# Order of the attention pairs in the local phase: the context tile's four short pairs first

## The reference

```python
o_mla = dense_attention(q_mla, k_mla, v_mla, MLA_SCALE)               # 8 heads
o_swa = window_attention(q_swa, k_swa, v_swa, kswa_c, vswa_c, sink, HEAD_SCALE)   # 4 heads, +-128 tokens
o_na = neighbourhood_attention(q_na, k_na, v_na, kna_c, vna_c, rpb, HEAD_SCALE)   # 4 heads, 2-D window
x = residual_tail(x, concatenate([o_mla, o_swa, o_na]), ...)
```

## Time and profile before

| | |
|---|---|
| time, median of 3 runs (lowest, highest) | 1341.08 us (1337.52, 1343.81) |
| profiled execution, span | 1336.3 us (the only time given for it) |
| PE busy | 1279.6 us, 96% |
| DVE busy | 613.7 us, 46% |
| ACT busy | 358.8 us, 27% |
| POOL busy | 152.5 us, 11% |
| mean granted TensorE clock of full speed | 0.991 |
| DMA | 313.16 MB, mean 234 GB/s |

### The profile page before, as it was taken

The page is one execution under the profiler, slowest core; times in us unless marked ns, Lnnn a source line. Parts: engine busy times, 40 slices in busy tenths (PEclk is TensorE's granted clock), DMA queues, the critical chain, the costliest instruction groups (busy, mean ns, idle before and its releaser), DMA issues. The chain is left out here.

```text
span 1336.3 us, 17216 instructions
## 1 busy us (share of the span) xinstructions
PE 1279.6 (96%) x6042; PEld 735.3 (55%) x6042; DVE 613.7 (46%) x1519; ACT 358.8 (27%) x931; POOL 152.5 (11%) x257
## 2 busy tenths in 40 slices
PE   6999999999999999999999999989999999999997
PEld 3555555565666564444455555566666656444443
DVE  0132266444566463433343224655556536344438
ACT  1121255434343210000012114563444311100001
POOL 2210220000000110000142003000000011000014
PEclk9999999998999999999999999999899999999999
DMA  9976996499111489999694038430201139999966
GB/s 355 363 248 220 347 332 254 162 359 327 42 64 64 168 333 398 361 374 367 260 334 161 16 140 291 151 128 15 88 33 64 63 130 352 404 368 360 362 270 246
DMA packets 125441, 313.16 MB, mean 234 GB/s; under 512 B 9882, under 2 KB 58426, under 8 KB 112688
## 3 DMA queue, kind: packets, MB, share of 16 engines
q1 hardware_dynamic: 90896, 243.13, 49.8%
q0 software_dynamic: 12848, 45.39, 9.0%
q10 hardware_dynamic: 21616, 23.60, 5.3%
HBM read 232.14 MB, written 80.71 MB: 234 GB/s over the span
## 5 line engine op out<-in xcount | busy, mean ns | idle before, releaser
L790 PE MATMUL ps<-ring,big 128*128 128x384 f32 (+2 forms) x640 | 230.7, 520 | 1.7 <-DVE big L1773 1.3
L790 PEld LDWEIGHTS ps<-ring,big 128*128 128x128 f32 x640 | 120.3, 190 | 104.6 <-issue 63.7
L871 PE MATMUL ps<-ring,arena 128*128 128x512 f32 x384 | 169.3, 594 | 1.9 <-ACT arena L1406 1.9
L502 PEld LDWEIGHTS ps<-consts,arena 128*128 128x128 f32 (+2 forms) x880 | 103.7, 143 | 79.1 <-issue 50.9
L502 PE MATMUL ps<-consts,arena 128*128 128x128 f32 (+2 forms) x880 | 129.7, 278 | 15.7 <-ACT arena L1227 6.6
L711 PE MATMUL ps<-ring,big 128*128 128x512 f32 x320 | 143.0, 598 | 0.8
L563 PE MATMUL ps<-arena 64*128 64x128 f32 (+5 forms) x576 | 137.9, 430 | 6.1 <-DVEq L1822 3.4
L1227 ACT ACTIVATE arena<-ps 128x384 f32<-128x384 f32 (+3 forms) x140 | 69.1, 493 | 221.3 <-PE ps L502 221.3
L871 PEld LDWEIGHTS ps<-ring,arena 128*128 128x128 f32 x384 | 71.2, 190 | 83.1 <-issue 83.1
L563 PEld LDWEIGHTS ps<-arena 64*128 64x128 f32 (+1 forms) x576 | 79.4, 196 | 65.8 <-issue 57.8
L711 PEld LDWEIGHTS ps<-ring,big 128*128 128x128 f32 x320 | 59.0, 190 | 70.4 <-issue 66.4
(11 more groups left out here) (237 smaller groups left out, 1481.9 us busy)
## 6 DMA issues: line engine op xcount, KB each, us to landing
ring<-in_w_mod SPq DMA_DIRECT2D x40, 1024.0 KB, 11.8
ring<-in_w_up SPq DMA_DIRECT2D x22, 1024.0 KB, 9.7
ring<-in_w_gate SPq DMA_DIRECT2D x22, 1024.0 KB, 7.6
slots<-zeros ACTq DMA_DIRECT2D x8, 2560.0 KB, 14.4
slots<-zeros SPq DMA_DIRECT2D x8, 2560.0 KB, 20.2
arena<-in_w_down SPq DMA_DIRECT2D x16, 1024.0 KB, 12.7
arena<-slots SPq DMA_DIRECT2D x30, 512.0 KB, 6.4
slots<-arena POOLq DMA_DIRECT2D x30, 512.0 KB, 9.6
```

The lines of the kernel that those rows point to most:

```text
L502: return pe.transpose(out, in_, ident)
L790: mm = pe.matmul(ps[:, c, 0:CHUNKS[c][1]], hT[:, s, k, :], slot[c][:, k, 0:CHUNKS[c][1]], start=(k == 0), stop=(k == KD - 1))
L871: mm = pe.matmul(ps[:, b, :], xgT[:, b, k * P:(k + 1) * P], w_gu[q][:, :, k, :], start=(k == 0), stop=(k == KD - 1))
```

## The change

The four pairs of the context tile stand at the head of the list instead of at its end. Nothing else in the code is edited.

```diff
             if phase == 2:
                 for c in range(2):
+                    out.append(dict(kind="swa", heads=(c, c + 2), t=4, c=c, chunk=4 + c, n=1, k=[(0, 640, 768)],
+                                    mask=[cst["swa"][:, P:2 * P]] * 2, v=[5]))
+                for c in range(2):
+                    out.append(dict(kind="ctx", heads=(2 * c, 2 * c + 1), t=4, c=c, chunk=6 + c, n=1, k=[(0, 640, 768)],
+                                    mask=[cst["swa"][:, P:2 * P]] * 2, v=[5]))
+                for c in range(2):
                     for t in range(4):
                         lo, hi = max(t - 1, 0), min(t + 1, 3)
...
                                         mask=[bias[:, 2 * c + h, j0:j0 + 512] for h in range(2)], v=[*range(5)]))
-                for c in range(2):
-                    out.append(dict(kind="swa", heads=(c, c + 2), t=4, c=c, chunk=4 + c, n=1, k=[(0, 640, 768)],
-                                    mask=[cst["swa"][:, P:2 * P]] * 2, v=[5]))
-                for c in range(2):
-                    out.append(dict(kind="ctx", heads=(2 * c, 2 * c + 1), t=4, c=c, chunk=6 + c, n=1, k=[(0, 640, 768)],
-                                    mask=[cst["swa"][:, P:2 * P]] * 2, v=[5]))
```

## The result

| | before | after |
|---|---|---|
| median of the runs | 1341.08 us (5 runs, 1337.52 to 1343.81) | 1350.04 us (5 runs, 1346.73 to 1356.61) |
| ratio, 95% interval | | 1.0078 [1.005, 1.0106] |
| span of the profiled execution, its mean clock | 1336.3 us, 0.991 | 1345.9 us, 0.991 |

What follows compares the result with a forecast made beforehand. PE, busy 96% of the span, was taken to bound the kernel. The local attention stages would grow 2.6 and 3.0, 5.6 us in all: span 1336.3 to 1341.9, with 4.8 more for the median 1346.7; range 1338 to 1355.

Steps and rivals of the forecast that it cites:

- The head: Start of each local attention stage: scores of pair 5 start at 18.2 us against 21.4, a gain of 3.2 per layer.
- the thin steps: Steps where PE works on one-block pairs beside DVE's full banded ones; the loop scores, maximum, next scores bounds them.
- the emptying: Four steps after pair 19's scores, with copies bare: 17.4 and 16.9 us by layer, against 8.3 before.
- The rival that it cancels: Whole kernel at 1342 us: same mechanism, scaling not held, loops of steps 5 to 9 shorter; chance 0.22.
- the held scaling: Step 2: POOL's second mask add holds DVE's scaling of pair 0, so the turn comes at 6.7, not 5.2 us.
- the rival that it is faster: Whole kernel at 1335 us: filling the pipeline costs, the drain is hidden; chance 0.08.
- The weights: First modulation group, first layer: both halves' weights arrive just in time, by 0.6 us; first half waits 0.8 if scaling is free.
- step 4: Near the stage's start: three-block scores, turn, values, half a modulation group, turn; 5.3 us.
- Steps 5 to 9: One-block turns and values beside full banded pairs, bound by the loop: 3.2, 3.2, 2.8, 3.35, 3.5, together 16.1 us.
- Steps 12 to 16: Neighbourhood scores: 4.1 us four times, one with modulation transposes 4.3, and 4.35; together 21.0 in the comparison table.
- The rival of the clock: Whole kernel at 1355 us: PE's clock falls in thin steps 5 to 7, adding 8 us; chance 0.15.
- my own conditions: A step is wrong if off over 0.5; forecast fails if clock falls in steps 5-9 or last scores come over 10 earlier.

Runs made afterwards that it cites:

- pairs in the middle: Kernel before, with the four short pairs between the banded and the neighbourhood pairs; 1350.79 us, ratio 1.0088.
- values between: Kernel before, with values(s - 4) computed between a step's two turns once no scores remain; 1335.95 us, ratio 0.9979; repeated 1335.83 us, 0.9994.
- groups later: Changed kernel with the three modulation groups at steps 5, 12 and 18 instead of 3, 10 and 17; 1349.32 us, ratio 1.0074.
- three remedies: Changed kernel with mask additions at positions 4, 5, 12, 13, values between the last turns, and modulation groups at steps 5, 12, 18; 1348.34 us, ratio 1.0076.
- fillers in the thin steps: Changed kernel with two more filling matmuls behind the scores in each of steps 5 to 8; 1350.96 us, ratio 1.0087.
- two pairs first: Only the two short swa pairs moved to the head, the two ctx pairs left at the end; 1338.72 us, ratio 1.0005.

## Why the prediction was right, and where it was short

- *Direction and mechanism.* The head gains, the thin steps give part of it back, the emptying costs more than both. Measured, in the first layer: -2.9, -1.7, -1.3, -0.5, +1.5, +11.4, sum +6.4 (forecast for the same lines -3.2, -2.6, -1.0, -1.2, +1.5, +9.1, sum +2.6). The run with the pairs in the middle separates the parts: no gain at the head and the same end. The rival that it cancels fell with the held scaling, and the rival that it is faster with the emptying.
- *The held scaling.* Right, with its price: 1.24 and 1.3 a layer by the kernel without it, where 1.5 was forecast. The row at 855.05 bears on it once more. The Trainium skill, "SBUF — State Buffer", section "Who interferes with whom", says that whichever issues first holds the shared ports for its whole instruction and the other blocks fully. The traces agree: 2.12 in place of 0.48, and 3.35 in place of 0.88, each ending 0.3 after the additions.
- *The weights.* Forecast: both halves just in time. The second waited 0.64, so step 4 of the first layer was 6.02 instead of 5.3. With the scaling free the first half waited 1.20 where 0.8 was forecast.
- *Steps 5 to 9 (16.1).* Short by 0.85 and 1.6. Two parts. In the second layer the clock fell in steps 7 and 8, about 0.9. And the modulation group has work on DVE too: its addition at 183.63 (L1665, 0.69 us) stands between two maxima, and step 6 was 3.93 instead of 3.2. I had priced the group only on PE. The number could have been read before the change: there the same addition stands between the same maxima, and the scores of steps 6 and 7 are 3.93 apart. In the kernel before, PE and DVE:

```profile
185.85 1.14 PE L563 MATMUL ps<-arena 64*128 64x384 f32 x8
...
189.78 0.92 PE L563 MATMUL ps<-arena 64*128 64x256 f32 x8
```

```profile
186.75 0.68 DVE L1665 TENSOR_TENSOR mrow<-ps,mrow 128x512 f32<-128x512 f32 x1
```

- *Steps 12 to 16 (21.0).* Short by 0.7 in both layers, of the same kind. Step 13 is 4.62 where 4.3 was forecast: beside the transposes on PE it has DVE's addition for the second group (L1665, 0.68 at 214.53). Step 15 is 4.48 where 4.1 was forecast, with DVE's copies of the transposes (L1687, at 223.51). Both lie in a loop that was already DVE's.
- *The emptying (17.4, 16.9).* Measured 19.7 and 17.6 to the end of the last values. The three copy waits, 1.87 and twice 0.79, are near the forecast's 1.9 and twice 0.87. A filling matmul takes about 0.5 there (258.35 to 258.88) where I had put 0.3 for each of three, 0.6 too little; four that take 1.93 had said so. In the first layer the clock fell from 253 to 257, which cost 1.6 by the three runs without that fall.
- *The rival of the clock.* I had it in steps 5 to 7 of each layer at 8 us in all and gave it 0.15. It came in other places and was worth 2.5. My argument against it, that 2.64 of 4 us busy had kept the full clock, was too short: thinner stretches came, 1.40 and 1.13 of 3. It then took back the remedies: six of the seven kernels with all four short pairs first (the changed one among them) had a low stretch inside a local stage, where neither the kernel before nor its version with values between had one.

By my own conditions, steps 4 (first layer), 6 and 7 (second layer) are off by 0.5 or more, and the fall in the second layer's thin steps is one that I had named as making the forecast fail; its 0.9 us did not.

That leaves the size: 5.6 forecast, about 9 to 9.6 measured. The local stages alone are +11.7, twice the forecast, of which 2.5 are clock; 2.5 came back in the stages between by a shorter low clock there. So that the measured time lies no further from the forecast is in part luck: two errors of one size and opposite sign, both of the clock. And by the prediction's own bounds for no change, 1334.4 to 1347.8, the measured 1350.04 is slower, to which it gave 0.40 against 0.52 for no change.

## What to carry to other kernels

In a software pipeline over items of unequal length, short items at the end are worth more than at the beginning: the last steps have nothing beside them, and their length is that of the last items on every engine. Count a step's work on every engine, the small modulation work on DVE here, and read the distances of the old trace for the steps that keep it. Look for positions in code that goes by the number in the list (POOL's additions) and not by what stands there. When a remedy frees TensorE in one place, ask whether the stretch before it becomes so thin that the clock falls; its gain may be gone.

## What the runs showed of the hardware

Every low clock inside a local stage came behind a few us in which PE was partly idle with the clock still at 1.00: 1.13 of 3 busy (250), 1.40 of 3 (837), 2.73 of 4 (169, groups later), 2.13 of 4 (202, three remedies); and 2.64 of 4 at 232 before the change was followed by none. The busy share of the stretch alone doesn't tell these cases apart. The emptying with fillers in the thin steps has the same 1.13 of 3 as the kernel after, at the same place of the same steps, and kept its clock:

```profile
251.00:254.00 3.00, 1.13 (x11) 0.72 (x11) 2.54 (x8) 1.73 (x5) 0.00 (x0) 1.00 1.05 398
254.00:258.00 4.00, 3.21 (x36) 2.67 (x34) 1.09 (x5) 1.75 (x4) 0.00 (x0) 1.00 1.05 387
```

Nor do the steps' lengths: the version with two pairs first had a low clock from 887 to 891, in step 18 of the second layer, and the one with only the values of the emptying moved, which is the same up to there, had none. What sets it apart stays open.

A whole kernel's time follows these stretches: one kernel's five runs from 1346.73 to 1356.61 us go with mean clocks from 0.992 to 0.983, about 1.1 us for 0.001. A difference of 1 us between medians is no evidence here; the distance between two scores in one layer repeats to 0.02 from run to run where neither the clock nor the code differs.
